# The low part of the projection weights on GpSimd instead of VectorE, in a two-block transformer kernel

## What is computed

```python
qkv = jnp.einsum('bld,de->ble', h, w_in)
q, k, v = jnp.split(qkv, 3, axis=-1)          # q, k: (L, 8 heads, 2, 64); v: (L, 8 heads, 128)
s = einsum('bqhcd,bkhcd->bhcqk', q, k) * scale + bias
p = jax.nn.softmax(s, axis=-1)
a = p[:, :, 0] - lam * p[:, :, 1]
o = einsum('bhqk,bkhe->bqhe', a, v)
o = _rmsnorm(o, subln_g) * (1.0 - lam_init)   # over the 128 columns of a head
m = einsum('ble,ed->bld', o, w_out)
```

## Time and profile before

| | |
|---|---|
| median of 3 runs | 2134.41 us (2129.05 to 2136.33) |
| the profiled execution | 2129.2 us, span 2127.4 us |
| mean granted TensorE clock | 0.958 |
| busy: PE, DVE, ACT, POOL | 94%, 50%, 32%, 8% of the span |
| chain that ended last, by engine | PE 82%, DVE 11%, issue 4%, ACT 3%, DMA and POOL 0% |

### The profile page before, as it was taken

One profiled execution on the slowest core, in us unless ns is written; L12 is line 12 of the kernel. 1 busy time (PEld: TensorE's weight loads), 2 busy tenths in 40 slices (PEclk: granted clock), 3 DMA queues, 4 the chain that ended last, 5 costly groups with the idle time before them and its releaser, 6 DMA issues.

```text
span 2127.4 us, 27654 instructions
## 1 busy us (share of the span) xinstructions
PE 1990.0 (94%) x11486; PEld 1737.7 (82%) x11486; DVE 1056.7 (50%) x1480; ACT 679.7 (32%) x958; POOL 175.9 (8%) x127
## 2 busy tenths in 40 slices
PE   7898888999999988998979999999989989999996
PEld 5677676888888777888869999999989877888885
DVE  7573645543434567565644534333375555343344
ACT  4443433322222335333323413222332233233231
POOL 3000003100000202000003100000210031000002
PEclk9996899999999999999988999999999999999998
DMA  4120102222222321011102122222212222222221
GB/s 168 60 84 35 50 1 79 81 98 99 99 99 79 119 80 60 21 60 41 44 37 80 60 100 100 79 99 81 97 60 100 90 89 79 91 97 89 99 99 40
DMA packets 25907, 166.07 MB, mean 78 GB/s; under 512 B 3792, under 2 KB 4048, under 8 KB 6352
## 3 DMA queue, kind: packets, MB, share of 16 engines
q1 hardware_dynamic: 25808, 164.66, 21.8%
HBM read 162.55 MB, written 2.10 MB: 77 GB/s over the span
## 4 chain that ended last, share of the span: by engine, by line
PE 82%; DVE 11%; issue 4%; ACT 3%; DMA 0%; POOL 0%; SPq 0%; DVEq 0%; ACTq 0%; POOLq 0%
PE ps L306 23%; PE ps L307 23%; PE ps L308 23%; DVE z_lo L413 2%; DVE ps L462 2%; PE ps L1806 2%; DVE w_lo L288 1%; PE ps L1572 1%; DVE h L475 1%; ACT w_hi L277 1%; PE ps L1807 1%; PE ps L1808 1%; PE ps L1574 1%; PE ps L1573 1%; PE ps L1840 1%
## 5 line engine op out<-in xcount | busy, mean ns | idle before, releaser
L306 PE MATMUL ps<-z_hi,w_hi 128*128 128x512 f32 (+1 forms) x1744 | 612.9, 351 | 50.4 <-DVE z_lo L413 34.9
L307 PE MATMUL ps<-z_lo,w_hi 128*128 128x512 f32 (+1 forms) x1744 | 608.3, 349 | 0.0
L308 PE MATMUL ps<-z_hi,w_lo 128*128 128x512 f32 (+1 forms) x1744 | 607.0, 348 | 0.0
L288 DVE TENSOR_TENSOR w_lo<-w_raw,w_hi 128x2048 fp32r<-128x2048 f32 x152 | 348.2, 2291 | 161.6 <-ACT w_hi L277 161.5
L277 ACT ACTIVATE w_hi<-w_raw 128x2048 fp32r<-128x2048 f32 x152 | 289.8, 1906 | 424.3 <-PE ps L308 413.7
L306 PEld LDWEIGHTS ps<-z_hi,w_hi 128*128 128x128 f32 x1744 | 333.9, 191 | 105.0 <-issue 32.7
L306 PE MATMUL ps<-arena,w_hi 128*128 128x256 f32 (+1 forms) x1144 | 385.2, 337 | 5.5 <-DVE arena L1189 5.5
L307 PE MATMUL ps<-arena,w_hi 128*128 128x256 f32 (+1 forms) x1144 | 385.2, 337 | 0.0
L308 PE MATMUL ps<-arena,w_lo 128*128 128x256 f32 (+1 forms) x1144 | 384.6, 336 | 0.0
L308 PEld LDWEIGHTS ps<-z_hi,w_lo 128*128 128x128 f32 x1744 | 333.8, 191 | 44.3
L307 PEld LDWEIGHTS ps<-z_lo,w_hi 128*128 128x128 f32 x1744 | 334.0, 192 | 42.7 <-issue 0.7
(11 more groups left out here) (261 smaller groups left out, 1940.4 us busy)
## 6 DMA issues: line engine op xcount, KB each, us to landing
w_raw<-wstream SPq DMA_DIRECT2D x152, 1024.0 KB, 4.8
h<-xT SPq DMA_DIRECT2D x8, 256.0 KB, 7.1
out<-h SPq DMA_DIRECT2D x8, 256.0 KB, 2.0
rope_cs<-pT SPq DMA_DIRECT2D x1, 512.0 KB, 5.5
acc<-pos SPq DMA_DIRECT2D x1, 256.0 KB, 2.7
acc<-lam SPq DMA_DIRECT2D x1, 128.0 KB, 8.5
sm<-small SPq DMA_DIRECT2D x1, 86.0 KB, 2.5
h<-metaT SPq DMA_DIRECT2D x1, 64.0 KB, 8.8
```

The source lines that it names most:

```text
L288: dve.tensor_tensor(w_lo[:, slot, :], w_raw[:, slot, :], w_hi[:, slot, :].bitcast(f32), ALU.subtract).then_inc(wlo, 1)
L306: pe.matmul(dst, wh, zh, start=(k == 0), stop=False)
L307: pe.matmul(dst, wh, zl, start=False, stop=False)
L308: last = pe.matmul(dst, wl, zh, start=False, stop=(k == nk - 1))
```

## The change

GpSimd makes the low part of the twelve blocks B_QKV + 2 to B_OUT2 + 1, each in four pieces of 512 columns; VectorE no longer does. GpSimd waits for `whi` as VectorE did, and for `wlo` of the block before, so that the count stays in order. In its loop the first conversion of iteration n stands ahead of the root of head n - 1, the second (m odd) behind it. VectorE waits once for GpSimd's last block, ahead of `out_tiles`.

```diff
             pool_sum(pool, 4, T, 0)
             pool.wait_ge(s("root_w"), 1)
-            for n in range(HEADS):
+
+            def pool_lo(b):
+
+                pool.wait_ge(whi, b + 1)
+                pool.wait_ge(wlo, b)
+                for a in range(0, BLK, 512):
+                    last = pool.tensor_tensor(w_lo[:, b % 2, a:a + 512], w_raw[:, b % 2, a:a + 512],
+                                              w_hi[:, b % 2, a:a + 512].bitcast(f32), ALU.subtract)
+                last.then_inc(wlo, 1)
+
+            def pool_root(n):
+
                 pool.wait_ge(s("d_e"), n + 1)
                 pool.tensor_tensor(cols[:, D_ROOT:D_ROOT + 5], cols[:, D_E:D_E + 5], root_w[:, :], ALU.pow).then_inc(s("d_root"), 1)
+            for n in range(HEADS):
+                m = n + 1
+                pool_lo(B_QKV + (3 * m + 1) // 2 if m % 2 else B_QKV + 3 * m // 2 + 1)
+                if n:
+                    pool_root(n - 1)
+                if m < HEADS and m % 2:
+                    pool_lo(B_QKV + (3 * m + 3) // 2)
+            pool_root(HEADS - 1)
             pool_sum(pool, 5, NLATE, LATE)
...
                 v_lo2(n)
-                w_next(B_QKV + (3 * m + 1) // 2 if m % 2 else B_QKV + 3 * m // 2 + 1)
 
                 d_min(u + 2, 0)
...
                     qk_lo(m, 0)
-                    if m % 2:
-                        w_next(B_QKV + (3 * m + 3) // 2)
...
             o_low(HEADS - 1)
+            dve.wait_ge(wlo, B_OUT2 + 2)
             out_tiles(B_OUT2, P_OUT2, NLATE)
```

## The result

The changed kernel takes 2154.31 us in the median of 8 runs (2142.97 to 2156.14), the kernel before, run beside it, 2133.61 (2127.82 to 2137.58). The ratio is 1.0088, with a 95% interval of 1.0065 to 1.0111: slower by 0.9%, some 20 us. The forecast was 2155, with a range from 2140 to 2174.

What follows compares the result with a forecast made beforehand. TensorE bounds the kernel, with slack only in the differential attention, where it waits for GpSimd and VectorE. Waits +20.3, clock +8, gain -7.5 make +20.8 us on the 2134.4 median: 2155, range 2140 to 2174.

Steps and rivals of the forecast that it cites:

- The term of the delay: Attention loop: GpSimd's conversion of 5.7 us makes TensorE wait for root and w_lo, 20.3 us together.
- its 17.5: TensorE's spread, iterations 1 to 7: each root 2.5 us late behind GpSimd's conversion, 17.5 us in all.
- The bounds of 5.1 and 7.0 us: Length of one four-piece conversion on GpSimd, taken as 5.7 us; the bounds give 16 and 31 us of waits.
- the lock rival: VectorE and GpSimd's pieces take turns at the shared port: conversion 7.0 us, 34 us slower, 2168; chance 0.14.
- -7.5: Gain where VectorE loses the second conversions and TensorE's scores come sooner: 7.5 us, at best 8.3.
- +8: Clock loss from TensorE's longer idle ahead of the spread: 1.0 us per iteration, 8 us; bounds nothing and 13.6.
- The clock doesn't mind: Rival: the slow-clock stretch ahead of the spread only slides into the idle; 13 us slower, 2147; chance 0.20.
- Faster than before: Rival: GpSimd finishes pool_lo so soon that the root is hardly late; 2126 with no delay; chance 0.06.
- break-even of 4.2 us: Length of GpSimd's four pieces at which, without clock loss, the root's delay equals the 8.3 us gain.
- The signs to look for: Traces in the attention if right: root behind the fourth piece, spread wait over 15 us, mean clock below 0.92.
- near 38: GpSimd's loop in the attention: roots at nearly equal steps near 38 us, none alternating.
- The cover for the later loads: SP issues w_raw of block b + 2 3.4 us later; its high part is due 13 us or more later: no cost.

Runs made afterwards that it cites:

- root-first: The change with GpSimd's root queued ahead of the first conversion instead of behind it: 2127.41 us against 2132.08 for the kernel before, ratio 0.9983.
- the powers: The kernel before, with four or seven needless 128x5 powers on GpSimd ahead of each root but the last: 2167.51 us (ratio 1.0167) and 2189.97 us (1.0278).
- the second conversions alone: The change with only the second conversions (four blocks) on GpSimd, the first ones kept on VectorE: 2124.29 us against 2132.08 before, ratio 0.9965.
- one-piece kernel: The change with one GpSimd instruction of 2048 columns per conversion in place of four of 512: 2142.48 us against 2133.79 before, ratio 1.0042.
- two profiles of the change: The second comes from the unchanged change, run again beside the last experiment: 2152.68 us against 2132.75 for the kernel before, ratio 1.0103.
- first conversions only: The change with only the first conversions (eight blocks) on GpSimd, the second ones kept on VectorE: 2150.55 us against 2132.08 before, ratio 1.0099.
- mixed: The change with the root first and the first conversions of odd m back on VectorE, eight blocks on GpSimd: 2118.13 us against 2133.79 before, ratio 0.9934.

## Why the prediction was right

**Place and sign.** The prediction read the root's place in GpSimd's queue as the cost, and that is what the runs show: root-first takes it away, the powers make it without any conversion moved, and the second conversions alone, with no conversion ahead of the root, are a gain.

**The term of the delay.** It took 5.7 us for a conversion and 20.3 us for the waits. The pieces took 1.25 to 1.34 us and a conversion 5.04; the rise of the waits was 21.1 us (19.0 at the spread, 2.1 for w_lo) in the first profile and 22.7 in the second. The price per conversion was 0.7 too high. By the prediction's own reckoning 5.04 us make a root 1.8 us late and 12.7 us at seven spreads; 19.0 were measured. That its 17.5 still came near is luck, an error the other way: TensorE was said to reach the spread as late as before. In iteration 2 it was there at 902.7, 2.9 us after w_hi; before it spread at 906.84, 4.4 us after w_hi, since it ran at 1.2 GHz up to there. Idle time partly took the place of slow matmuls. The bounds of 5.1 and 7.0 us missed 5.04 by a hair, and the lock rival's 7.0 was not seen; the 4497 ns that the Trainium skill ("GPSIMD Engine Reference", "Elementwise — side-by-side cycle accounting") gives for one sum of 2048 columns is near the 4.56 us of the one-piece kernel's subtraction.

**The terms of gain and clock.** As single terms, -7.5 and +8 don't hold. The gain of the second conversions is 7.8 us only where the root is on time, and most of it is clock, not idle time; beside the late root nothing of it shows. The clock's 8 us for the late root were 4.4 and 3.8 net in two profiles of the change, 9.8 and 5.8 in the two kernels with powers, and none with the first conversions only. Added up they still fit: forecast were about +16 us of idle (20.3 less the 4.2 of the row minimum) and +4.7 of clock; the stage shows +15.5 and +4.4, then +17.1 and +3.8.

**The rivals.** "The clock doesn't mind" gave 2147 and lies just outside: the interval of the ratio begins at 1.0065 (2147.5). The stages of the change speak against it too (3.8 and 4.4 us of clock), that of first-only for it, so it was rejected for the sum, not in every kernel. "Faster than before" needed four pieces in 4.2 us; they took 5.04. Its break-even of 4.2 us was reached by no run; at 4.56 us per conversion the cost had already fallen to 8.7 us, which points that way.

**The signs to look for.** Four pieces with the root right behind, over 15 us at the spread, a wait for w_lo in iteration 0 (2.1 us), one w_lo left on VectorE, a mean clock below 0.92 (0.91): all there. The steps of the loop are 37.8, 37.8, 39.3, 39.0, 39.4 and 39.0 us, without the alternation of the earlier trace rows; "near 38" was a little low. VectorE's d_mix did take longer beside the pieces (1.62 us for 400 columns), but its 2 us of slack covered that. One reading was wrong without effect: the two closest conversions are not 13 us apart but 9.7 (833.96 and 843.62, in iteration 0 of the kernel before). The cover for the later loads is longer in any case, since w_raw of block b + 2 is needed only two conversions on; the next but one after 833.96 is at 867.66.

**What stays open.** In which iterations the clock falls was read off, not explained, and so the clock's part of each cost was measured as a sum over one or two profiles. The 11 us between mixed and root-first are shown only in part. A root raised by VectorE itself, right behind the mean and with all twelve conversions on GpSimd, was planned with the other experiments and expected to be 6 to 10 us faster than before; it gave no time, so nothing is known of it.

## What to carry to other kernels

An engine that is 8% busy can still be on the path: before giving it work, list what others wait for from it, and put the new work behind the short, urgent instruction, not ahead of it. Ask of each moved piece when its reader wants it: here eight of twelve conversions had slack and are worth 15.7 us on GpSimd, four had none and belong where they are made fastest. When halves of a change are measured alone, don't expect them to add: a late step can hide what an earlier wait cost, and the clock moves with both.

## What the runs showed of the hardware

A GpSimd instruction of five columns and 1.17 us took 3.22 us beside VectorE's 2048-column instruction with two SBUF inputs, and got on only when that was nearly over; VectorE's 400-column TENSOR_SCALAR took 1.62 us beside GpSimd's pieces and 0.49 without. Four GpSimd subtractions of 512 columns cost 5.04 us, one of 2048 columns 4.56; from these I estimate 0.16 us for each further start. And the granted clock can give or take nearly as much as the waits do: of the 29.1 us between the stages of the change and of root-first, which hold the same instructions (307.8 and 278.7), 16.1 are idle time and 13.8 clock (the rest differs by 0.7 the other way).
